# A decoder layer's last 24 microseconds: pairs of token tiles, and row work shared anew among DVE, ACT and POOL

## What is computed

```
def moe(h, ...):
    ...
    down = lax.ragged_dot(clamped_swiglu(up), w_down, group_sizes) + b_down[e_sorted]
    out = jnp.zeros_like(hf).at[tok].add(down * g_sorted[:, None].astype(down.dtype))

def reference(...):
    ...
    y = moe(h, w_router[l], b_router[l], w_up[l], b_up[l], w_down[l], b_down[l])
    x = x + gt_f * rms_norm(y, g_post_ffn[l])

def rms_norm(x, g):
    y = xf * lax.rsqrt(jnp.mean(xf * xf, axis=-1, keepdims=True) + RMS_EPS)
    return (y * g.astype(jnp.float32)).astype(x.dtype)
```

## Time and profile before

| | |
|---|---|
| time, median of 3 runs | 1423.92 us (1423.67 to 1424.4) |
| profiled execution: span from first to last instruction | 1418.3 us |
| what lies around the span, median less span | 5.6 us |
| instructions | 45734 |
| granted clock of the core over the span, mean | 0.984 of full |
| last 24 us: first scatter product | 1398.13 us |
| first output issued | 1411.02 us |
| end of the span | 1418.3 us |

### The profile page before, as it was taken

How to read it: one execution, slowest core, us unless ns; L and a number is a source line. 1 busy time by engine, 2 the same in 40 slices (tenths; PEclk the granted TensorE clock), 3 DMA queues, 4 the chain that set the end, 5 groups by cost and what they waited for, 6 DMA issues and landing times.

```text
span 1418.3 us, 45734 instructions
## 1 busy us (share of the span) xinstructions
PE 1291.5 (91%) x18541; PEld 756.0 (53%) x18542; DVE 626.0 (44%) x1752; ACT 347.8 (25%) x868; POOL 312.8 (22%) x421
## 2 busy tenths in 40 slices
PE   6999999999989998978989977799999999998994
PEld 3464555665556555544545534455555555554552
DVE  2567646885474333332333323333334433332345
ACT  2121005773231222211212211122222222221222
POOL 0400003553002222211222211122222222222222
PEclk9999999999999999999999989999999999999997
DMA  9777404004799999999999999999989989999997
GB/s 352 267 260 258 161 0 179 2 2 165 296 360 389 386 410 418 427 421 422 417 422 402 404 427 429 418 418 415 420 330 423 395 336 397 420 424 429 408 423 315
DMA packets 66079, 483.89 MB, mean 341 GB/s; under 512 B 9708, under 2 KB 16660, under 8 KB 45304
## 3 DMA queue, kind: packets, MB, share of 16 engines
q1 hardware_dynamic: 57616, 465.56, 79.4%
q0 software_dynamic: 8144, 17.78, 4.8%
q10 hardware_dynamic: 280, 0.02, 0.0%
HBM read 467.78 MB, written 19.93 MB: 344 GB/s over the span
## 4 chain that ended last, share of the span: by engine, by line
PE 67%; DMA 26%; DVE 4%; issue 2%; ACT 1%; SPq 1%; DVEq 0%; POOL 0%; POOLq 0%
PE ps L2016 26%; DMA arena<-in_w_down 24%; PE ps L2036 15%; PE ps L1665 9%; PE ps L1909 4%; PE ps L1805 2%; PE ps L1773 2%; PE ps L1839 2%; DMA arena<-in_w_in 1%; PE ps L1632 1%; PE ps L2024 1%; DMA arena<-token_numbers 1%; PE ps L1644 0%; PE ps L1652 0%; PE ps L1703 0%
## 5 line engine op out<-in xcount | busy, mean ns | idle before, releaser
L2016 PE MATMUL ps<-arena 128*32 128x256 f32 x10240 | 584.0, 382 | 45.7 <-issue 29.4
L2016 PEld LDWEIGHTS ps<-arena 128*32 128x32 f32 x10240 | 339.1, 111 | 267.3 <-issue 55.2
L2036 PE MATMUL ps<-arena 128*32 128x256 f32 x5120 | 302.5, 387 | 35.9 <-DMA arena<-in_w_down 35.4
L1494 DVE TENSOR_SCALAR arena<-ps 128x128 f32<-128x128 f32 x160 | 46.6, 291 | 565.2 <-PE ps L2024 560.0
L958 ACT ACTIVATE arena<-ps,arena 32x256 f32<-32x256 f32 x316 | 147.6, 467 | 384.6 <-DMA token_sums<-arena 235.3
L2036 PEld LDWEIGHTS ps<-arena 128*32 128x32 f32 x5120 | 155.0, 111 | 160.1 <-issue 45.9
L699 POOL DMA_INDIRECT arena<-xn_rows,arena x82 | 85.8, 1046 | 408.0 <-DVE arena L1455 265.5
L691 POOL DMA_INDIRECT token_sums<-arena x80 | 110.9, 1387 | 221.9 <-ACT arena L958 218.9
L949 ACT ACTIVATE arena<-arena 128x128 f32<-128x128 f32 x160 | 49.5, 310 | 384.7 <-DVE arena L1494 384.6
L1665 PE MATMUL ps<-arena 128*128 128x512 f32 (+1 forms) x320 | 127.9, 555 | 0.0
L1665 PEld LDWEIGHTS ps<-arena 128*128 128x128 f32 x320 | 59.7, 190 | 59.6 <-issue 55.0
(11 more groups left out here) (339 smaller groups left out, 962.5 us busy)
## 6 DMA issues: line engine op xcount, KB each, us to landing
arena<-in_w_up SPq DMA_DIRECT2D x67, 2048.0 KB, 15.4
arena<-in_w_down SPq DMA_DIRECT2D x64, 2048.0 KB, 29.3
arena<-in_w_up SPq DMA_DIRECT2D x30, 4096.0 KB, 26.7
arena<-in_w_ada SPq DMA_DIRECT2D x11, 2048.0 KB, 11.9
arena<-in_w_in SPq DMA_DIRECT2D x5, 2048.0 KB, 10.0
arena<-in_w_o SPq DMA_DIRECT2D x2, 2048.0 KB, 11.0
arena<-in_x SPq DMA_DIRECT2D x4, 512.0 KB, 5.0
arena<-in_w_ada SPq DMA_DIRECT2D x2, 1024.0 KB, 11.9
```

What stands on the lines that cost most here:

```text
L2016: ins = pe.matmul(out_of(y, g), xgT[:, 2 * n + k, :], tiles[par][n][:, k, at:at + 256], start=(n == 0 and k == 0), stop=False)
L2036: ins = pe.matmul(out_of(5, g), actT[:, y, k, :], tiles[par][4 + y][:, k, 256 * g:256 * (g + 1)], start=False, stop=(y == 1 and k == 3))
```

## The change

All of it concerns what comes after the last expert chunk, but for the renaming in its first part.

1. The four token tiles become two **pairs**. `y_ps` puts tiles 0 and 1 into PSUM banks 0 to 3, tiles 2 and 3 into banks 4 to 7, and PE signals each pair (`y_tail[0]`, `y_tail[1]`), so that the row sums of a pair wait for its products alone.
2. ACT takes the root after each pair of squares, and DVE makes the norm steps for each pair.
3. The gain products are shared anew: POOL makes those of tiles 0, 1 and 3, DVE that of tile 2.
4. The last row of tile 1 (`BY_POOL`) moves from DVE (one instruction) to ACT (scale) and POOL (add of x2).
5. The x2 read of tile 0 is issued before the wait for the token sums, those of 1, 2, 3 behind the reads of the token sums. Outputs are issued in the order 0, 2, 1, 3.
6. Several semaphores of the front part are merged into ones that count further (`hid_ps`, `hid_dve`, `cmp_ps`, `cmp_dve`); each wait stands where it stood.

```
-        y_ps = [ps[:, i // 2:8:2, 256 * (i % 2):256 * (i % 2) + 256] for i in range(NT)]
-        FIN_ORDER = (0, 2, 3, 1)
+        y_ps = [ps[:, i // 2 * 4:i // 2 * 4 + 4, 256 * (i % 2):256 * (i % 2) + 256] for i in range(NT)]
+        BY_POOL = 1
...
-        POOL_GAINS = 2
+        POOL_GAINS = (0, 1, 3)
+        TAIL_RSTD = 7
...
@@ SP
+            def x2_rows(i):
+                sp.dma_start(x2fin[:, i, :], x2_d[P * i:P * (i + 1)]).then_inc(x2_in[i], 16)
+
+            x2_rows(0)
             sp.wait_ge(written, (total - 1) * 16 + FILLED)
             for i in range(NT):
                 sp.dma_start(acc_in[:, i, :], acc_d[P * i:P * (i + 1)]).then_inc(fin_in[i], 16)
-            for i in FIN_ORDER:
-                sp.dma_start(x2fin[:, i, :], x2_d[P * i:P * (i + 1)]).then_inc(x2_in[i], 16)
-            for n, i in enumerate(FIN_ORDER):
-                sp.wait_ge(fin_dve, n + 1)
+            for i in range(1, NT):
+                x2_rows(i)
+            for i, done, count in ((0, fin_dve, 1), (2, fin_dve, 2), (1, fin_pool, 1), (3, fin_dve, 3)):
+                sp.wait_ge(done, count)
                 sp.dma_start(out[i * P:(i + 1) * P, :], result[:, i, :]).then_inc(out_done, 16)
@@ POOL
-            for i in range(POOL_GAINS):
+            for i in POOL_GAINS:
                 pool.wait_ge(row_sums, i + 1)
                 pool.tensor_tensor(gained_y[:, i, :], acc_in[:, i, :], gbf_fin, ALU.mult).then_inc(gain_ready, 1)
+            pool.wait_ge(scaled_tail, 1)
+            pool.wait_ge(x2_in[BY_POOL], 16)
+            pool.tensor_tensor(result[:, BY_POOL, :], gained_y[:, BY_POOL, :], x2fin[:, BY_POOL, :], ALU.add)\
+                .then_inc(fin_pool, 1)
@@ ACT
+            act_e.wait_ge(ms_ready, NORM_ALL + 1)
             for i in range(NT):
...
-            act_e.wait_ge(ms_ready, NORM_ALL + 1)
-            act_e.activation(fin[:, 8:12], fin[:, 0:4], ACT.Sqrt, scale=1.0 / D, bias=fin[:, 19:20])
-            act_e.activation(fin[:, 4:8], fin[:, 0:4], ACT.Identity, scale=1.0 / D, bias=fin[:, 19:20])\
-                .then_inc(root_ready, 1)
+                if i % 2:
+                    act_e.activation(fin[:, 7 + i:9 + i], fin[:, i - 1:i + 1], ACT.Sqrt, scale=1.0 / D, bias=fin[:, 19:20])
+                    act_e.activation(fin[:, 3 + i:5 + i], fin[:, i - 1:i + 1], ACT.Identity, scale=1.0 / D,
+                                     bias=fin[:, 19:20]).then_inc(root_ready, 1)
+            act_e.wait_ge(tail_chain, TAIL_RSTD)
+            act_e.wait_ge(gain_ready, 1 + POOL_GAINS.index(BY_POOL))
+            act_e.activation(gained_y[:, BY_POOL, :], gained_y[:, BY_POOL, :], ACT.Copy,
+                             scale=fin[:, 8 + BY_POOL:9 + BY_POOL]).then_inc(scaled_tail, 1)
@@ DVE
-            v.wait_ge(y_tail, 4)
             for i in range(NT):
+                v.wait_ge(y_tail[i // 2], 4)
                 v.wait_ge(fin_in[i], 16)
...
-            for i in range(POOL_GAINS, NT):
-                tstep(v.tensor_tensor(gained_y[:, i, :], acc_in[:, i, :], gbf_fin, ALU.mult))
-            ms, r, half = [fin[:, at:at + NT] for at in (4, 8, 12)]
-            v.wait_ge(root_ready, NORM_ALL + 1)
...
-            for i in FIN_ORDER:
...
+            tstep(v.tensor_tensor(gained_y[:, 2, :], acc_in[:, 2, :], gbf_fin, ALU.mult))
+
+            def tail_rstd(pair):
+                ms, r, half = [fin[:, at + 2 * pair:at + 2 * pair + 2] for at in (4, 8, 12)]
+                v.wait_ge(root_ready, NORM_ALL + 1 + pair)
...
+            tail_rstd(0)
+            assert tail[0] == TAIL_RSTD
+            final_rows(0)
+            tail_rstd(1)
+            final_rows(2)
+            final_rows(3)
@@ PE
-                    if i == NT - 1:
-                        ins.then_inc(y_tail, 1)
+                    if i % 2:
+                        ins.then_inc(y_tail[i // 2], 1)
```

More of the change, by code:

```diff
@@ L359, in hybrid_layer @@
             sem(n) for n in ("pj_ps", "pj_ev", "roped", "tg_ps", "tg_ev", "ab_ready")]
[L360 to L364, removed]
+        blk_ready, hid_ps, gel_in, gel_out, hid_dve = [
+            sem(n) for n in ("blk_ready", "hid_ps", "gel_in", "gel_out", "hid_dve")]
+        HID_PRODUCT, HID_TURNED, HID_KV = 1, 2, 3
+        HID_GELU, HID_COPIED, HID_KV_COPIED = 1, 2, 3
+        cmp_ps, cmp_dve, sc_exp = [sem(n) for n in ("cmp_ps", "cmp_dve", "sc_exp")]
+        CMP_SCORES, CMP_TURNED = 1, 2
+        CMP_SHIFTED, CMP_PROBS, CMP_COPIED = 1, 2, 3
         qk_done, neg_ready, exp_done, scl_ready, scaled_act, scaled_pool = [
@@ L396, in hybrid_layer @@
         out_done, tail_chain = sem("out_done"), sem("tail_chain")
-        fin_dve, gain_ready, row_sums, last_out, y_tail = [
-            sem(n) for n in ("fin_dve", "gain_ready", "row_sums", "last_out", "y_tail")]
+        fin_dve, fin_pool, scaled_tail, gain_ready, row_sums, last_out = [
+            sem(n) for n in ("fin_dve", "fin_pool", "scaled_tail", "gain_ready", "row_sums", "last_out")]
+        y_tail = [sem("y_tail0"), sem("y_tail1")]
         x2_in = [sem(f"x2_in{i}") for i in range(NT)]
@@ L463, in slot_used @@
                 kind, m = RING[n][0]
-                done, count = {"ada": (ada_ps if m < PE_ADA else row_sb, ADA_AT.get(m, 0) + 1), "in": (pj_ps, NT * (m + 1)), "c1": (hid_u, 1),
+                done, count = {"ada": (ada_ps if m < PE_ADA else row_sb, ADA_AT.get(m, 0) + 1), "in": (pj_ps, NT * (m + 1)), "c1": (hid_ps, HID_PRODUCT),
                                "wo": (wo_ps, 2 * (2 * NT - 1 + m))}[kind]
@@ L1203, in _ @@
                 ins = v.tensor_copy(hidv[:, :, g], src)
-            ins.then_inc(hid_sb, 1)
-            v.wait_ge(cv_ps, 1)
+            ins.then_inc(hid_dve, 1)
+            v.wait_ge(hid_ps, HID_KV)
             for u in range(2):
@@ L1223, in _ @@
             link(v.tensor_reduce(m32, s_view, AX.X, ALU.max, negate=True))
-            v.tensor_tensor(p_view, s_view, bc(m32, 2, 32), ALU.add).then_inc(sc_in, 1)
+            v.tensor_tensor(p_view, s_view, bc(m32, 2, 32), ALU.add).then_inc(cmp_dve, 1)
             gain_diag(0, 0, 2)
@@ L1538, in _, with final_rows @@
             v.wait_ge(row_sums, NT)
-            for i in range(POOL_GAINS, NT):
-                tstep(v.tensor_tensor(gained_y[:, i, :], acc_in[:, i, :], gbf_fin, ALU.mult))
-            ms, r, half = [fin[:, at:at + NT] for at in (4, 8, 12)]
-            v.wait_ge(root_ready, NORM_ALL + 1)
[L1543 to L1547, removed]
-            for i in FIN_ORDER:
-                if i < POOL_GAINS:
-                    v.wait_ge(gain_ready, i + 1)
+            tstep(v.tensor_tensor(gained_y[:, 2, :], acc_in[:, 2, :], gbf_fin, ALU.mult))
+            def tail_rstd(pair):
+                ms, r, half = [fin[:, at + 2 * pair:at + 2 * pair + 2] for at in (4, 8, 12)]
+                v.wait_ge(root_ready, NORM_ALL + 1 + pair)
+                tstep(v.reciprocal(r, r))
+                tstep(v.tensor_tensor(half, r, r, ALU.mult))
+                tstep(v.tensor_tensor(half, half, ms, ALU.mult))
+                tstep(v.tensor_scalar(half, half, -0.5, 1.5, ALU.mult, ALU.add))
+                tstep(v.tensor_tensor(r, r, half, ALU.mult))
+            def final_rows(i):
+                if i in POOL_GAINS:
+                    v.wait_ge(gain_ready, 1 + POOL_GAINS.index(i))
                 v.wait_ge(x2_in[i], 16)
-                v.scalar_tensor_tensor(out=result[:, i, :], in0=gained_y[:, i, :], scalar=r[:, i:i + 1],
+                v.scalar_tensor_tensor(out=result[:, i, :], in0=gained_y[:, i, :], scalar=fin[:, 8 + i:9 + i],
                                        in1=x2fin[:, i, :], op0=ALU.mult, op1=ALU.add).then_inc(fin_dve, 1)
+            tail_rstd(0)
[4 more added lines that the diff above has]
+            final_rows(3)
         @block.tensor
@@ L1778, in first_scores @@
             def first_scores():
-                pe.wait_ge(cv_sb, 1)
+                pe.wait_ge(hid_dve, HID_KV_COPIED)
                 pe.wait_ge(gb_sb, 2)
@@ L1785, in _ @@
             pe.wait_ge(roped, 5)
-            pe.wait_ge(sc_in, 1)
+            pe.wait_ge(cmp_dve, CMP_SHIFTED)
             pe.wait_ge(gb_sb, 4)
```

40 lines of the change are left out of this document (20 added, 20 removed).

## The result

The changed kernel took 1426.91 us (median of 14 executions), the one before 1425.06 us in the same sessions. The ratio is 1.0016, 95% interval 1.0009 to 1.0023: 2.3 us slower (between 1.3 and 3.3; the plain medians differ by 1.85), inside the 0.2% that the prediction called no change, though the interval excludes zero. The prediction said +2.3 us and a time of 1426.2; that time is 0.7 us short because it stands on 1423.92, a median of 3 executions of the kernel before, which over 14 is 1.1 higher. One execution of the kernel with both cures took 7176.83 us and is counted in no ratio.

A forecast was written before the change was run, and what follows sets the result against it. PE had 67% of the chain, but only the last 24 us counted, ended by an unbroken run of outputs. Data end 1419.3 - 1417.0 = +2.3; span 1420.6 plus 5.6 gives 1426.2 us, range 1423.2 to 1428.2.

The forecast's parts named there:

- part 1: Scatter products in pairs: first pair done at 1399.32, row sum 0 starts at 1399.35, 0.9 us earlier.
- part 2: Tile 0's x2 read ahead of the token sums: they land 0.5 later; last row sum starts 1403.8, ends 1405.0.
- part 3: POOL's gain products: first starts at 1400.74, two end at 1405.42; the third, released at 1405.0, queues behind them.
- part 4: DVE's one gain product is held to 1405.42 and ends 1406.50; POOL's third then ends at 1408.54.
- part 5: Norm steps of pair 0 on DVE: second step held to 1408.6, end at 1409.2, 0.5 gained.
- part 7: Row 1: ACT's scale ends 1410.3; POOL's add gets its turn at 1410.53 for 2.04, to 1412.57.
- part 8: Norm steps of pair 1 on DVE: held to 1412.6, done 1413.25; remaining outputs, including finished row 1, wait.
- part 9: Last row 2 ends 1414.58; outputs 2, 1, 3 form one unbroken run ending 1419.3, against 1417.0 before.
- the price: Short norm-step product meeting a POOL instruction: taken as POOL's whole turn, 2.04 us, with bounds 0 and 2.04.
- Rival D: Front x2 read slows the last scatter of rows to 8.5; token sums 1.3 later; 1426.8 to 1428.2; chance 0.2.
- B: Short norm-step products slip between POOL's turns: +0.6, time 1424.5 us; chance 0.17.
- C: No contention of POOL and DVE at all behind the last expert: 1.5 faster, 1422.4 us; chance 0.05.

The follow-up runs named there:

- both cures: The changed kernel with mean and half term of the norm steps in PSUM and outputs in the order 0, 1, 2, 3; ratio 0.9996 to the kernel before.
- the memset run: The kernel before plus one POOL memset of 128x2048 into unused memory beside the norm steps; executed once, no ratio, stretch from first scatter product to end 21.3 us.

## Why the prediction was right

Taken by its own parts, each as the distance from the first scatter product (1398.13 in the profile before, 1398.67 after):

| part | end of | forecast | measured |
|---|---|---|---|
| 1 | start of row sum 0 | 1.22 | 1.26 |
| 2 | row sum 3 | 6.87 | 6.81 |
| 3 | start of POOL's products | 2.61 | 2.65 |
| 4 | DVE's gain product | 8.37 | 8.40 |
| 4 | POOL's third product | 10.41 | 10.60 |
| 5 | norm steps of pair 0 | 11.07 | 11.21 |
| 7 | POOL's add | 14.44 | 14.81 |
| 8 | norm steps of pair 1 | 15.12 | 15.44 |
| 9 | last row 2 | 16.45 | 16.75 |
| 9 | data of the outputs (run of three) | 21.2 | 21.5 |

- **The mechanism** is shown, by taking it away in four ways (steps in PSUM, gain row in PSUM, either POOL instruction removed) and by adding it to a kernel that did not have it. The first held step goes with POOL's third product, the second with its add.
- **The row that carried the price was the wrong kind.** I took the whole turn for a short product because L1087 was held, but L1087 is a tensor_scalar with one SBUF input, and the memset run shows that this form can be held where a product passes. That the price held nonetheless was partly luck. A row of the right kind was in the trace before, though the prediction says that there is none: a product of 128x2 with two SBUF inputs, L1258, took 0.27 where most of its line take 0.16, and ended 0.02 behind a POOL product (another did so at 272.66).

```profile
289.23 1.27 POOL L666 TENSOR_TENSOR arena<-arena 128x512 f32<-128x512 f32 x1 [0.71 <-ACT arena L857]
...
290.24 0.27 DVE L1258 TENSOR_TENSOR arena<-arena 128x2 f32<-128x2 f32 x1
```

- **The size** was 0.36 us short in the stretch (22.47 against 22.83). The mis-sized term is POOL's turn behind DVE: I took 2.34 - 0.3 = 2.04 from the turns at 54 us, and it was 2.20 for the third product (1407.07 to 1409.27) and 2.28 for the add (1411.20 to 1413.48), so 0.16 and 0.24 more, together a little over the 0.36. The 0.3 came from a length for 768 columns that was itself worked out; DVE's L1540 before, at the size in question, gained only 0.14 by its turn (1.22 alone, 1.08 behind POOL), as POOL's third product did (2.34 and 2.20). ACT's scale, 1.15 against 1.06, added nothing.
- **The x2 read** (part 2): its 0.5 for the last token sum is not shown. The 6.81 of the table fits it, but the five other kernels with the read in front have 6.0 to 6.4, so that agreement is luck. It costs nothing at the end either way, because POOL's second product sets DVE's gain product. Rival D had a mechanism that did not occur.
- **Rivals B and C** are out: both L1563 were held for the whole turn.
- **The order of the outputs** (part 8, SP waits for row 2 ahead of row 1) costs 1.4 of the 2.7 us by itself. With the order put right, moving row 1 back to DVE, and with it POOL's add away, gives 0.7 more; taking the third product away, with the order as it was, gives 0.6. The effects overlap, since the run of outputs begins at last row 2, so they need not add up.
- **The forecast of no change** held by the bound of 0.2%, with the interval now resolving a slowdown that the bound did not; the sum had said slower all along.
- Left open: the 0.5 us of the profiles' difference that lies ahead of the scatter products. The loop of experts differs by as much and more between profiles of all these kernels (their first scatter product starts from 1396.73 to 1403.57), and no edit here touches it. The kernel with both cures has all of the renamed semaphores of part 6 and comes to 0.9996 (0.9983 to 1.0009), so no cost of them shows.

## What to carry to other kernels

When work is shared between DVE and POOL, ask of each DVE instruction beside a long POOL one whether both its inputs lie in SBUF, not how long it is: a step of 0.16 us took 2.18. If they must overlap, give the DVE instruction a PSUM operand (the wait then moves on to the next DVE instruction with two SBUF inputs), or keep POOL quiet while a chain of short dependent steps runs. And where results are written as they are made, put the finished tile first into the queue: the end is the last gap in the output plus the tiles behind it.

## What the runs showed of the hardware

- A DVE product of 128x2 or 128x4 with both inputs in SBUF waited for the end of the POOL product, add or copy of 128x1024 beside it (at 290 us also of 128x512), to within 0.02 us. With one input in PSUM it takes 0.17, and a 128x1024 one 1.22.
- Beside very small POOL instructions no such hold shows: at 63.4 to 64.1 us of the kernel before, three scalar_tensor_tensor of 128x32 with two SBUF inputs took 0.20 to 0.25 among POOL casts of 128x128 to 128x1 and a tensor_scalar of 128x4, whose rows read 0.43 to 0.58, and 0.20 or 0.21 at 61.5 to 62.2 without them.
- Which form is held depends on POOL's: beside a POOL memset the products passed in 0.17 and the short tensor_scalar with one SBUF input was held 1.25 (one execution). The reciprocal, one SBUF input, was never held, as at 1407.11 (0.17) beside POOL's third product. The Trainium skill ("SBUF — State Buffer", section "Who interferes with whom") says that a DVE instruction with two SBUF inputs contends with a POOL instruction that reads SBUF and not with one that only writes, and that tensor_scalar can enter a two-port mode, which contends with POOL without that condition. The trace agrees with the first (0.87 beside the copy, 0.17 beside the memset); the 1.25 fits the second, but no row tells in which mode the tensor_scalar ran. Neither of my two readings before the memset run had this.
- Wherever a DVE instruction with two SBUF inputs and a long POOL product or add both stood ready in these last 24 us, they took turns, one each, and a POOL instruction that waits for its turn shows the wait in its own length: the third product of the changed kernel, begun beside DVE's gain product, reads 3.31 and the add in the kernel with its steps in PSUM 3.22, instead of 2.34 to 2.36.
